# Seven block products in the second half of a feed-forward layer, in twelve of its 24 blocks

## The reference, cut to what matters

```python
h2 = rms_norm(x, norm2_g) * (1 + sc2) + sh2
x = x + g2 * (jnp.square(jax.nn.relu(h2 @ w_ff1)) @ w_ff2)   # 1024 -> 4096 -> 1024, float32
```

## Time and profile before

| | us |
|---|---|
| median of 3 runs | 2657.52 |
| their range | 2654.63 to 2658.02 |
| the profiled execution's own time | 2655.8 |
| its span, first to last instruction | 2654.0 |

### The profile page before, as it was taken

One profiled execution on the slowest core, in us unless ns is written; L12 is line 12 of the kernel. 1 busy time (PEld: TensorE's weight loads), 2 busy tenths in 40 slices (PEclk: granted clock), 3 DMA queues, 4 the chain that ended last, 5 costly groups with the idle time before them and its releaser, 6 DMA issues.

```text
span 2654.0 us, 45790 instructions
## 1 busy us (share of the span) xinstructions
PE 2565.2 (97%) x16346; PEld 2276.6 (86%) x16346; DVE 1742.6 (66%) x3965; ACT 1200.1 (45%) x3012; POOL 1130.1 (43%) x774
## 2 busy tenths in 40 slices
PE   7999989998999899998999999999999999999998
PEld 4778857886777547887999999999999999999998
DVE  4268889988999557886755555565555557555555
ACT  4343313558888435555333334434433343443332
POOL 0000000008998025565545445545545454555553
PEclk8999999998999999999999999999999999999999
DMA  7867625834444884654235333543443345244222
GB/s 294 284 211 237 205 104 193 282 123 133 140 138 156 334 305 162 210 181 147 93 113 174 113 118 119 160 135 104 164 140 130 96 137 170 87 157 162 80 64 84
DMA packets 309615, 427.04 MB, mean 161 GB/s; under 512 B 23098, under 2 KB 238886, under 8 KB 302854
## 3 DMA queue, kind: packets, MB, share of 16 engines
q1 hardware_dynamic: 287514, 374.69, 42.4%
q0 software_dynamic: 4272, 39.19, 4.2%
q10 hardware_dynamic: 17604, 10.24, 1.3%
HBM read 351.63 MB, written 144.55 MB: 187 GB/s over the span
## 4 chain that ended last, share of the span: by engine, by line
PE 48%; DVE 3%; issue 1%; DMA 0%; SPq 0%; ACT 0%; POOL 0%; DVEq 0%; POOLq 0%; ACTq 0%
PE ff_u_ps L3303 11%; PE ff_u_ps L3305 11%; PE ff_u_ps L3304 11%; PE opening_ps L3303 5%; PE opening_ps L3305 5%; PE opening_ps L3304 5%; DMA gluT<-h_d 0%; PE ff_out_ps L3298 0%; DVE ff_wT L3160 0%; DVE ff_h_lo L3131 0%; DVE ff_h_hi L3128 0%; SPq L2868 0%; DVE ff_wT L3121 0%; DVE ff_wT L3123 0%; DVE ff_wT L3119 0%
## 5 line engine op out<-in xcount | busy, mean ns | idle before, releaser
L2952 POOL TENSOR_TENSOR ff_w_lo<-gluT,ff_w_hi 128x512 fp32r<-128x512 f32 x293 | 395.7, 1357 | 338.8 <-ACT ff_w_hi L3000 338.4
L3000 ACT ACTIVATE ff_w_hi<-gluT 128x512 fp32r<-128x512 f32 x293 | 181.7, 627 | 256.3 <-PE ff_u_ps L3305 160.3
L2952 POOL TENSOR_TENSOR ff_w_lo<-ff_wT,ff_w_hi 128x512 fp32r<-128x512 f32 x144 | 193.9, 1348 | 225.1 <-ACT ff_w_hi L3000 164.9
L3303 PE MATMUL ff_u_ps<-ff_a_hi,ff_w_hi 128*128 128x352 f32 (+1 forms) x880 | 282.0, 320 | 5.8 <-POOL ff_a_lo L2967 3.1
L3304 PE MATMUL ff_u_ps<-ff_a_lo,ff_w_hi 128*128 128x352 f32 (+1 forms) x880 | 281.9, 320 | 0.0
L3305 PE MATMUL ff_u_ps<-ff_a_hi,ff_w_lo 128*128 128x352 f32 (+1 forms) x880 | 281.7, 320 | 0.0
L3203 DVE SCALAR_TENSOR_TENSOR ff_y<-ff_u_ps,modT,ff_y 128x352 f32<-128x352 f32 (+2 forms) x224 | 125.6, 570 | 212.7 <-PE ff_u_ps L3305 212.5
L3000 ACT ACTIVATE ff_w_hi<-ff_wT 128x512 fp32r<-128x512 f32 x144 | 90.6, 632 | 273.3 <-PE ff_u_ps L3305 128.8
L1776 ACT ACTIVATE pa_score<-pa_score,pa_stat 128x256 f32<-128x256 f32 (+1 forms) x384 | 172.3, 451 | 31.8 <-DVE pa_stat L1718 29.4
L3303 PE MATMUL ff_u_ps<-ff_h_hi,ff_w_hi 128*128 128x352 f32 (+1 forms) x524 | 168.8, 322 | 3.2 <-issue 1.6
L3303 PEld LDWEIGHTS ff_u_ps<-ff_a_hi,ff_w_hi 128*128 128x128 f32 x880 | 165.5, 188 | 7.2 <-POOL ff_a_lo L2967 3.6
(11 more groups left out here) (494 smaller groups left out, 7380.1 us busy)
## 6 DMA issues: line engine op xcount, KB each, us to landing
gluT<-in_w_ff_dram SPq DMA_DIRECT2D x192, 512.0 KB, 5.0
out_new_k_sample_dram<-in_cache_k_dram SPq DMA_DIRECT2D x40, 511.0 KB, 6.1
out_new_v_sample_dram<-in_cache_v_dram SPq DMA_DIRECT2D x40, 511.0 KB, 6.2
dwq<-in_w_ada_dram SPq DMA_DIRECT2D x32, 512.0 KB, 8.8
gluT<-in_cache_k_dram SPq DMA_DIRECT2D x16, 1024.0 KB, 8.8
gluT<-h_d SPq DMA_DIRECT2D x80, 176.0 KB, 4.5
accs<-acc_d SPq DMA_DIRECT2D x16, 768.0 KB, 8.4
out_new_k_sample_dram<-in_cache_k_dram POOLq DMA_DIRECT2D x3, 4088.0 KB, 16.8
```

The source lines that it names most:

```text
L2952: pool.tensor_tensor(slot_view(w_lo, s), src, slot_view(w_hi, s).bitcast(F32), ALU.subtract).then_inc(w_lod, 1)
L3000: act.activation(slot_view(w_hi, s), src, ACT.Copy).then_inc(w_hid, 1)
L3303: pe.matmul(out, w_hi[s % WR][:, w], hi, start=first, stop=False, skip_group_check=more)
```

## The change

Blocks 1 to 6 of runs 1 and 2 (`SEVEN`, twelve blocks) make the down half by seven block products as well. The 2x2 blocks are: hidden tiles of pair 0 against pair 1, token half 0 against token half 1, output tiles 0 to 3 against 4 to 7. Each of the seven products has four groups (`k`) of two hidden tiles, six matmuls each: 28 groups and 14 slots in place of 16 groups and eight slots.

- The operands A11, A22 and A12 are blocks of activations; S3, S1, S2 and S4 are sums. DVE makes eight sums (`seven_sum`), ACT the high parts (`a_high`, `sum_high`), DVE 14 low parts (`seven_low_part`) in place of eight.
- The weight sums are made once, in run 0. `t_sums` are stored to DRAM (`tu_d`) and only run 0 makes them; `td_sum` makes sums of w_ff2 in blocks 1 to 6 of run 0 and they are stored too (`td_d`). Runs 1 and 2 load either by slot.
- The product sums 1, 6 and 7 are kept in `e167`, the others in the quarters of `y`. `accumulate_seven` adds without the gate. In a run's last block seven `combine` additions put them together on DVE and ACT applies the gate (`gate`, 16 instructions); after the plain block one subtraction (`fx_d`) corrects a quarter of `y`.
- In runs 1 and 2 weights are requested by slot (256 KB) into a ring of six (`RAW`), each when the slot six before it has been made low. A copy part is requested at every sixth slot. Residual rows, stores and pieces of h2 get places in this order by slot number. The residual rows share memory with `e167`, `wT` and `td`.

A cut diff, with its leading spaces shortened:

```diff
+SEVEN = [b >= BLKS and 0 < b % BLKS < BLKS - 1 for b in range(NB_ALL)]
+DOWN_SLOTS = [14 if x else KT for x in SEVEN]
+DOWN_GROUPS = [28 if x else DN for x in SEVEN]
...
+RAW = 6
...
+DOWN_OPS = (("A11", None, 1), ("S3", 2, 7), ("A22", 3, 4), ("A12", None, 2), ("S1", 0, 5), ("S2", 1, 6), ("S4", None, 3))
+OPS_READY = (2, 4, 6, 8, 10, 12, 14)
...
+e167 = sb("e167", [P, 3, 4, W])
+shared = e167[:].rearrange("p a k t -> p (a k t)")
+wT = shared[:, 0:4 * 512].rearrange("p (n c) -> p n c", n=4)
+td = [flat_glu[:, 4 * D:4 * D + 4 * 512].rearrange("p (n c) -> p n c", n=4), shared[:, 4 * 512:8 * 512].rearrange("p (n c) -> p n c", n=4)]
...
-x1_own = sb("x1_own", [P, 2, D])
+x1_own = shared[:, 4 * 512:4 * 512 + 2 * D].rearrange("p (a c) -> p a c", a=2)
...
+    if b >= BLKS:
+        r = (s - S_OWN) % RAW
+        eng.wait_ge(raw_in[r], 16 * sum(raw_loads(n) for n in range(S_OWN + r, s + 1, RAW)))
+        return flat_glu[:, r * 512:(r + 1) * 512]
...
+def operand(tiles, sums, name, h, w):
+    if name in ("S1", "S2"):
+        return sums[:, (2 if name == "S2" else 0) + h, 0:w]
+    f, c = {"A11": (2 * h, 0), "S4": (2 * h, 0), "S3": (2 * h, 1), "A12": (2 * h + 1, 0), "A22": (2 * h + 1, 1)}[name]
+    return tiles[:, f, c * w:(c + 1) * w]
+def seven_low(b, n):
+    return (("A11", 0), ("A11", 1), ("S3", 0), ("S3", 1), ("A12", 0), ("A22", 1), ("A22", 0), ("A12", 1),
+            ("S1", 1), ("S1", 0), ("S2", 1), ("S2", 0), ("S4", 0), ("S4", 1))[n]
+LOW_ORDER = (0, 1, 2, 3, 5, 6, 4, 7, 8, 9, 10, 11, 12, 13)
...
+def product_sum(n, w):
+    if n in (1, 6, 7):
+        return e167[:, {1: 0, 6: 1, 7: 2}[n], :, 0:w]
+    half, c = {2: (0, 0), 3: (1, 0), 4: (0, 1), 5: (1, 1)}[n]
+    return y[:, 4 * half:4 * half + 4, c * w:(c + 1) * w]
...
+        def load_slot(s):
...
+            if s - S_OWN >= RAW:
+                sp.wait_ge(w_lod, s - RAW + 1)
...
+            (name, n, _), q = DOWN_OPS[m // 2], m % 2
+            if n is not None:
+                sp.dma_start(dst, td_d[blk - 1, q, :, TD_PLACE[n]]).then_inc(raw_in[r], 16)
+            else:
...
+        def load_sums(blk, q):
...
+        def store_sums(blk, q):
+            sp.wait_ge(td_s[q], 4 * blk)
+            sp.dma_start(td_d[blk - 1, q], td[q]).then_inc(td_out[q], 16)
+        def store_up(blk, j):
+            sp.wait_ge(t_d, 4 * (2 * (blk - 1) + j + 1))
+            sp.dma_start(tu_d[blk - 1, j], wT).then_inc(tu_out, 16)
...
+        for s in range(S_OWN, NSLOT):
+            b, i = locate(s)
             run, blk = divmod(b, BLKS)
             last = (run - 1) * TR
...
+            if s == S_OWN + 8:
+                sp.wait_ge(tu_out, 16 * 2 * (BLKS - 1))
+            load_slot(s)
+            if blk and i % 6 == 3:
+                next_part()
+            if blk == 0 and i == 5:
                 load_h(run, 2)
                 load_h(run, 3)
...
+            if blk == 0 and i == 12:
+                store(last)
+                store(last + 1)
+                load_x1(last + 2)
+                load_x1(last + 3)
                 load_h(run, 6)
...
+            if blk == 0 and i == 13:
+                store(last + 2)
+                store(last + 3)
+                load_x1(last + 4)
+                load_x1(last + 5)
                 load_h(run, 7)
-            if blk == 1 and t == 0 and run:
...
+            if blk == 1 and i == 0:
                 load_h(run, 8)
                 load_h(run, 9)
...
-            if blk == 6 and t == 0 and run < NR - 1:
+            if blk == BLKS - 1 and i == 13 and run < NR - 1:
+                sp.wait_ge(u_pe, STEP0[b])
                 load_h(run + 1, 0)
                 load_h(run + 1, 1)
...
+            if SEVEN[b] and j == 0 and t in (1, 2):
+                return
...
+        def sum_high(b, n):
+            w = RUNS[b // BLKS][1]
+            name, h = seven_low(b, n)
+            act.wait_ge(ss_d, SUM0[b] + {2: 1, 3: 2, 8: 3, 9: 4, 10: 5, 11: 6, 12: 7, 13: 8}[n])
+            if n == 12:
+                act.wait_ge(u_pe, up_done(b) + 4)
+            act.activation(operand(a_hi, s_hi, name, h, w), seven_source(name, h)[:, 0:w], ACT.Copy).then_inc(ahi_d, 1)
+        def gate(run, d):
...
+            act.wait_ge(cm_d, 7 * (run - 1) + (4 if k < 4 else 7))
+            view = y[:, k, c * w:c * w + min(w, SEQ - t0 - c * w)]
+            act.activation(view, view, ACT.Copy, scale=modT[:, M_G2 + k, 8:9]).then_inc(gt_d, 1)
...
+                if SEVEN[b] and j == 1 and o == 1:
+                    sum_high(b, 2)
+                    sum_high(b, 3)
...
+                if run and blk == BLKS - 1 and j == 1 and o >= 3:
+                    gate(run, 2 * o - 6)
+                    gate(run, 2 * o - 5)
...
+                if run and blk == BLKS - 1 and 3 <= k < 7:
+                    gate(run, 2 * k + 2)
+                    gate(run, 2 * k + 3)
+                if SEVEN[b]:
+                    for n in {1: (8,), 2: (9,), 4: (10, 11), 8: (12,), 9: (13,)}.get(k, ()):
+                        sum_high(b, n)
...
+            if q:
+                v.wait_ge(tu_out, 16 * q)
...
+        def td_sum(blk, q, n):
...
+            out, a, b = ((0, 1, 0), (1, 3, 1), (3, 3, 0), (2, 2, 3))[n]
+            v.tensor_tensor(td[q][:, out], td[q][:, a], td[q][:, b], ALU.subtract).then_inc(td_s[q], 1)
+        def seven_sum(b, n):
+            w = RUNS[b // BLKS][1]
...
+            out, x, x2, op = ((z[0], z[0], z[2], ALU.subtract), (z[3], z[3], z[1], ALU.subtract),
+                              (z[1], z[1], zz[1], ALU.add), (z[2], z[2], zz[2], ALU.add),
+                              (z[3], zz[1], z[3], ALU.subtract), (z[0], zz[2], z[0], ALU.subtract),
+                              (zz[0], zz[0], z[0], ALU.subtract), (zz[3], zz[3], z[3], ALU.subtract))[n]
+            v.tensor_tensor(out[:, 0:w], x[:, 0:w], x2[:, 0:w], op).then_inc(ss_d, 1)
+        def seven_low_part(b, n):
+            w = RUNS[b // BLKS][1]
...
+            v.tensor_tensor(operand(a_lo, s_lo, name, h, w), seven_source(name, h)[:, 0:w],
+                            operand(a_hi, s_hi, name, h, w).bitcast(F32), ALU.subtract).then_inc(alo_d, 1)
+        def combine(run, n):
+            w = RUNS[run][1]
+            v.wait_ge(cm_d, 7 * (run - 1) + n) if n else v.wait_ge(y_d, Y0[run * BLKS + BLKS - 1])
+            out, x = ((6, 1), (2, 1), (7, 6), (4, 7), (6, 5), (5, 7), (3, 6))[n]
+            v.tensor_tensor(product_sum(out, w), product_sum(out, w), product_sum(x, w), ALU.add).then_inc(cm_d, 1)
+        def accumulate_seven(b, d):
...
+            if blk == 1:
+                v.wait_ge(fx_d, run)
+                if d == 0:
+                    for i in range(2):
+                        v.wait_ge(out_s[i], 16 * 3 * run)
+            dst = product_sum(n, w)[:, k]
+            if blk == 1 and n in (1, 6, 7):
+                v.tensor_copy(dst, src).then_inc(y_d, 1)
+            else:
+                v.tensor_tensor(dst, src, dst, ALU.add).then_inc(y_d, 1)
...
+            if run and blk == 0:
+                v.tensor_copy(y[:, k, c * w:(c + 1) * w], src).then_inc(y_d, 1)
+                return
+            if run:
+                v.wait_ge(gt_d, DN * (run - 1) + d + 1)
...
+                merge = run and blk == BLKS - 1
+                if run == 0 and j == 0:
                     t_sums(b, 1)
+                if merge and j == 0:
+                    combine(run, 0)
...
+                if SEVEN[b] and j == 1:
+                    seven_low_part(b, 1)
+                    seven_sum(b, 0)
+                    seven_sum(b, 1)
+                    seven_low_part(b, 2)
+                if merge and j:
+                    combine(run, 3)
+                elif merge:
+                    combine(run, 1)
+                    combine(run, 2)
...
+                if SEVEN[b] and j == 1:
+                    seven_low_part(b, 3)
...
-                relu(1, q, w)
-                a_low(e)
+                relu(1, w, zj)
+                if not SEVEN[b]:
+                    a_low(e)
+                elif j == 0:
+                    seven_low_part(b, 0)
...
-                relu(2, q, w)
-                a_low(e + 1)
+                relu(2, w, zj)
+                if not SEVEN[b]:
+                    a_low(e + 1)
+                elif j:
+                    seven_low_part(b, 4)
...
-                relu(3, q, w)
-                a_low(e + 2)
-                a_low(e + 3)
+                relu(3, w, zj)
+                if not SEVEN[b]:
+                    a_low(e + 2)
+                    a_low(e + 3)
+            if SEVEN[b]:
+                seven_sum(b, 2)
+                accumulate_seven(b, 0)
+                seven_low_part(b, 5)
+                accumulate_seven(b, 1)
+                seven_sum(b, 3)
+                accumulate_seven(b, 2)
+                seven_low_part(b, 6)
+                accumulate_seven(b, 3)
+                accumulate_seven(b, 4)
+                seven_low_part(b, 7)
+                accumulate_seven(b, 5)
+                seven_sum(b, 4)
```

(91 more changed lines are left out.)

204 lines of the change are left out of this document (143 added, 61 removed).

## The result

The changed kernel takes 2627.3 us (median of 4 runs, 2625.9 to 2632.9), the kernel before 2656.3 us in the same comparison (4 runs, 2654.6 to 2658.0). The ratio is 0.9894, with a 95% interval of 0.9882 to 0.9906: faster by 29 us, or 1.1%. The prediction was 2641, range 2614 to 2664.

What follows compares the result with a forecast made beforehand. TensorE's matmul count was taken to bound the blocks. Twelve blocks gain 15.9 us, less 0.9 for `combine` and gates, plus 1.5 for an earlier h2 piece: 16.5, giving 2641 us, range 2614 to 2664.

Steps and rivals of the forecast that it cites:

- The prize: Twelve down halves: 24 fewer matmuls each, saving 3.82 us per block in run 1, 3.67 in run 2; 44.9 in all.
- Holds make S4's low parts late: Changed down halves: DVE and POOL operations exclude each other, so S4 starts 2.1 us late in run 1.
- low parts at a mean near 0.88: Sign to look for in the changed kernel: DVE's low parts still average near 0.88 us.
- The milder reading: DVE and POOL only share bandwidth: operations 0.37 us longer, last operand some 0.4 late, result near 2614.
- Run 2: Its six changed blocks: S4 2.5 us late plus 1.0 at three bank waits, leaving 0.75 gained per block.
- Supply and bookkeeping: `t_sums` stalls vanish (0.2 us per run 1 block, 0.6 in run 2); earlier h2 piece gains 1.5.
- Loads by slot: Weight requests through the six-slot ring: taken as 0 us lost, bounds 0 to 25 over 49 copies.
- `combine` and gates: Last down halves of runs 1 and 2: additions and gates lose 0.3 and 0.6 us, bounds zero to 3 each.
- (b): Rival: full gain, S4 in time because DVE's order falls into POOL's gaps; 2607, up to 2622; chance 0.14.
- (a): Likeliest case: the queue layout with late S4 holds, 2628 to 2652 us; chance 0.58.
- (c): Rival: slower, accumulates and low parts queue behind held sums, banks and operands late; 2674 at 5.4 us stalls; chance 0.12.
- (d): Rival: slot loads come late or run 0 pays for its stores; 10 to 25 us back, 2650 to 2667; chance 0.16.

Runs made afterwards that it cites:

- e4: Changed kernel without the seven products (16 groups in every down half), keeping loads by slot, stored up-half weight sums and the new request order; 2643.1 us, ratio 0.9951.
- e5: Changed kernel with DVE's sums, low parts and accumulates reordered a second time, bank drains as late as the six banks allow, nothing left out; 2602.5 us, ratio 0.9801.
- e3: Changed kernel with POOL's weight low part cut to 128 of 512 columns in the twelve down halves (computation changed), DVE order kept; 2603.6 us, ratio 0.9802.
- e2: Changed kernel with DVE's sums, low parts and accumulates placed in a first new order laid out by the rule of holds; 2607.0 us, ratio 0.9817.
- e6: Changed kernel with accumulates 21 and 22 put ahead of S4's two low parts on DVE; 2658.1 us, ratio 1.0012 to the kernel before.
- e7: Changed kernel with S4's two low parts put behind accumulate 23 on DVE; 2661.7 us, ratio 1.0025 to the kernel before.
- e1: Changed kernel with DVE making S4's two low parts ahead of accumulates 19, 20 and 21; 2612.6 us, ratio 0.9834 to the kernel before.

## Why the prediction was right

The mechanism and its place came true. The sizes were off, mostly to one side: 27.9 us were gained behind the first `p1s` where 16.5 were forecast, and the slower clock, which took 3 back, was not in the sum at all.

**The prize**: 24 matmuls at 0.159 and 0.153. Right: TensorE's count is 12 x 24 lower, and from e4's blocks (57.58, 55.30) to e5's (53.80, 51.65) it is 3.78 and 3.65 us per block, against 3.82 and 3.67. (336 x 0.159 is 53.4, not 53.6 as written there; nothing in the sum hangs on it.)

**Holds make S4's low parts late.** Right in mechanism and place: twelve waits, at the first matmul of S4, for a DVE low part. In run 1 the stand was laid out at 2.1 us and is 1.8; blocks of 55.8 were predicted and 55.71 came, though 55.8 is the layout's own 57.7 for before, less 1.9; from the real 58.03 it is 2.3 less. The layout held line by line: in the block shown, counted from the start of its down half (1908.87, 24 groups of 0.955 before 1931.79), `seven_sum` 4 ran from 8.6 to 10.1 (laid out 8.7 to 10.2), the last two low parts from 22.0 to 23.2 and from 23.5 to 24.7 (laid out 22.3 to 23.4 and 23.8 to 24.9). The sign "low parts at a mean near 0.88" was too low: the two groups under e3 show 1.09 and 0.96 in the changed kernel. By the Trainium skill, page "SBUF — State Buffer" (Who interferes with whom), a DVE operation on two SBUF inputs and a POOL operation that reads SBUF take turns. That held: DVE's low parts shrink from means of 0.96 and 1.09 to 0.52 and 0.62 when POOL's work does, with nothing else changed (e3). The milder reading that I weighed, shared bandwidth with S4 0.4 late, is refuted by the stand of 1.8 and by single operations of 1.58 and 1.59 us in the rows of DVE, each ending 0.38 behind the end of a POOL operation.

**Run 2** is the term that was mis-sized. The working had S4 2.5 late and 1.0 more at three bank waits, 3.5 in all. It came to 2.08, with no bank wait, so a block won 2.0 where its clock held (55.84, the mean of five blocks before, to 53.87), instead of 0.75. Here each matmul is 0.006 us shorter while POOL's 1.30 is the same; I followed four queues, and the three bank waits did not come. That such waits lie near is shown by e2, where they appeared at 0.2 us each.

**What the prediction didn't foresee** is the clock. In two of run 2's six blocks the first twelve matmuls after the stand went at 0.28 us instead of 0.153, 1.5 us lost each.

**Supply and bookkeeping** was taken at 4.8 for the stalls behind `t_sums` and 1.5 for the earlier piece of h2, 6.3. The part without the seven products is worth 12.3 (e4). The stall of run 1 is 0.25 and not 0.2, and e4's block is 0.45 shorter (57.58 against 58.03): 0.33 is the stall with the late matmul behind it, and the rest lies in steps between matmuls, such as 24 steps of 0.167 at the start of the down half before (block of the earlier trace rows), which are 0.16 in e4. The stretches around the plain blocks gave 2.7 us in the changed kernel. No DVE wait for a piece of h2 is left in them, where the earlier trace rows had 8.4 us; from 1700 to 2600 us this is the only wait for a DMA on any engine of the changed kernel:

```profile
ACT ff_h_hi L3184 <- DMA gluT<-h_d: 3.5, 2, 2.7
```

Why those steps became shorter was not tried.

**Loads by slot cost nothing.** Right. 256 KB land in 3.0 to 3.4 us, and ACT waits for no weight load in runs 1 and 2. The DMA issues of the changed kernel (count, KB, us to landing), to be read against the earlier trace rows:

```profile
gluT<-in_w_ff_dram SPq DMA_DIRECT2D x196, 256.0 KB, 3.4
...
gluT<-tu_d SPq DMA_DIRECT2D x112, 256.0 KB, 3.0
gluT<-td_d SPq DMA_DIRECT2D x96, 256.0 KB, 3.2
...
out_new_v_sample_dram<-in_cache_v_dram SPq DMA_DIRECT2D x40, 511.0 KB, 5.4
```

**`combine` and gates**: laid out at 0.3 and 0.6. In the last blocks of runs 1 and 2 TensorE stands 0.37 and 0.62 us for a low part of POOL, which neither the kernel before nor e4 shows there. Not foreseen: the end behind the last matmul is 13.4 us instead of 12.75.

The account, predicted and measured (span 2654.0 to 2624.0):

| | predicted | measured |
|---|---|---|
| run 1, six blocks | 11.4 | 14.7 |
| run 2, six blocks | 4.5 | 10.0 (13 without the clock) |
| plain blocks and their neighbours | 1.2 | 2.7 |
| run 0 | 0 | 1.6 |
| end | -0.6 | -1.0 |
| stages before (profile to profile) | 0 | 2.1 |
| sum | 16.5 | 30.0 |

(Rounded one by one.) The 2.1 us of the stages before are no part of what was forecast: over the nine profiles the first `p1s` starts anywhere from 1299.5 to 1306.3 us.

And the seven products alone, from e4 to the changed kernel (1339.9 to 1324.3 us from the first `p1s`): 15.6 of 44.9. Stands before S4 took 6 x 1.81 + 6 x 2.08 = 23.3. Slow matmuls after them took 4.2: 3.1 in the two stretches at half clock, and 0.1 at the first matmul behind each of the other stands. That leaves 1.8 for `combine`, gates and the end. With e5's order (1297.4) 42.5 of 44.9 arrive. So the full gain, rival (b), was there to be had, though not in the order as written; (a) is what happened, though 2627.3 lies just beyond the fast end of its 2628 to 2652. Rivals (c) and (d) did not: no bank waits, and e4 is faster and not slower. For (c), e6 and e7 show how near it lay.

## What to carry to other kernels

When a trade removes TensorE work and adds element work, totals per block (DVE 40 of 54 us here) say little: lay the queues out in time with the holds between DVE and POOL in them, and look at the last operand that TensorE needs. Placing one operand's two low parts two and three accumulates earlier was worth 15 us here and the best order 25, without one instruction more or less. And give one engine's burst a place where the other stands anyway.

## What the runs showed of the hardware

**A stand of TensorE can take half of its clock away for the matmuls behind it.** The changed kernel, second block of run 2, in order of time:

```profile
2332.26 0.64 PE L3646 MATMUL opening_ps<-ff_a_hi,ff_w_hi 128*128 128x336 f32 x1 [1.93 <-DVE ff_a_lo L3403]
2332.70 0.48 PE L3647 MATMUL opening_ps<-ff_a_lo,ff_w_hi 128*128 128x336 f32 x1
2332.98 0.48 PE L3648 MATMUL opening_ps<-ff_a_hi,ff_w_lo 128*128 128x336 f32 x1
...
2335.76 0.32 PE L3646 MATMUL ff_u_ps<-ff_a_hi,ff_w_hi 128*128 128x336 f32 x1
2335.92 0.31 PE L3647 MATMUL ff_u_ps<-ff_a_lo,ff_w_hi 128*128 128x336 f32 x1
```

and the stretch of it, with the granted clock in the third last column:

```profile
2332.20:2336.00 3.80, 3.74 (x14) 3.74 (x15) 1.39 (x5) 0.04 (x1) 1.15 (x1) 0.55 0.77 265
```

The step from one matmul to the next is 0.28 there, and 0.153 after it: a granted clock of 0.55, near the 1.2 GHz level, and then 2.4 again. After stands before S4 of 0.55 to 0.85 us this followed in none of 12 blocks (e1), after 1.8 in none of 6, after 2.1 to 2.2 in 2 of 8 (changed kernel and e6), after 3.0 to 3.3 in 21 of 22 (e6, e7), in run 1 as in run 2. So it goes with the length of the stand and not with run 2's tiles. It costs 1.4 to 1.7 us, in 7 of the 21 cases 2.6 to 3.0. In e7 slow matmuls cost 23 us against 4 in the changed kernel, 19 more, while the stands themselves grew by 15: late low parts cost more than their lateness. Why two of the six alike stands of 2.1 us were followed by it and four not, and why one of 3.3 us was not, stays open.

**Holds alternate.** Under POOL operations on end, DVE operations on two SBUF inputs mostly wait for the POOL operation that runs (1.1 to 1.6 us in place of 0.51), and POOL operations lose time to DVE's: e5's six in 8.71 us are 1.45 each instead of 1.30.
